# A state-space layer between two feed-forward layers: dt inside the projection, and a scan with its decays made another way

## What is computed

```python
zxbcdt = h @ w_in                              # 1024 -> 2048 (z) + 4096 (x, B, C) + 32 (dt)
xbc = silu(causal_dwconv(xbc, conv_w, conv_b))
dt = softplus(dt + dt_bias);  A = -exp(A_log)
for each chunk of 128 tokens:
    acum = cumsum(dt * A)
    lmat = exp(where(mask, acum[l] - acum[s], -inf))
    y_diag = einsum(C·B * lmat, x * dt)
    y_off = einsum(C, state) * exp(acum)
    state = state * exp(acum[-1]) + einsum(B, x * dt * exp(acum[-1] - acum))
y = (y_diag + y_off + x * D) * silu(z)
y = rms_norm(y per group of 256 channels) * norm_g
out = y @ w_out
```

## Time and profile before

| | us |
|---|---|
| median of 3 runs (lowest to highest) | 3338.79 (3338.55 to 3340.55) |
| the profiled execution, its own time | 3345.62 |
| its span, first to last instruction | 3343.8 |
| mean granted TensorE clock | 0.933 |
| TensorE busy | 3082.7 (92%) |
| VectorE busy | 2405.0 (72%) |
| ScalarE busy | 1660.4 (50%) |
| GpSimd busy | 123.0 (4%) |

### The profile page before, as it was taken

The page is one execution under the profiler, slowest core; times in us unless marked ns, Lnnn a source line. Parts: engine busy times, 40 slices in busy tenths (PEclk is TensorE's granted clock), DMA queues, the critical chain, the costliest instruction groups (busy, mean ns, idle before and its releaser), DMA issues. The chain is left out here.

```text
span 3343.8 us, 58689 instructions
## 1 busy us (share of the span) xinstructions
PE 3082.7 (92%) x23865; PEld 2754.2 (82%) x23865; DVE 2405.0 (72%) x3656; ACT 1660.4 (50%) x2382; POOL 123.0 (4%) x178
## 2 busy tenths in 40 slices
PE   7679999899888899999988899999999998988899
PEld 6567778689877789898976899899789898878798
DVE  6569999688775468787577578786578788674555
ACT  4437777554552354544552444544554544442444
POOL 0010000000102000000000000000000001011000
PEclk8779999899999799999986899999999999998899
DMA  9347999667410267586430377674157586300442
GB/s 382 140 170 288 400 402 373 247 262 310 178 64 4 95 249 305 219 313 265 155 137 1 120 298 281 257 306 178 74 229 306 221 314 260 116 2 3 166 182 80
DMA packets 77519, 698.09 MB, mean 209 GB/s; under 512 B 8433, under 2 KB 12657, under 8 KB 55409
## 3 DMA queue, kind: packets, MB, share of 16 engines
q1 hardware_dynamic: 30928, 525.06, 39.8%
q10 hardware_dynamic: 42912, 157.31, 12.4%
q0 software_dynamic: 3456, 12.58, 1.0%
HBM read 690.72 MB, written 4.19 MB: 208 GB/s over the span
## 5 line engine op out<-in xcount | busy, mean ns | idle before, releaser
L1075 PE MATMUL banks<-u_split,w_split 128*128 128x512 f32 x2816 | 1014.7, 403 | 23.3 <-DVE u_split L1320 21.2
L1144 ACT ACTIVATE w_split<-ring 128x1024 fp32r<-128x1024 f32 x513 | 541.4, 1058 | 672.6 <-PE banks L1076 408.8
L1251 DVE TENSOR_TENSOR w_split<-ring,w_split 128x1024 fp32r<-128x1024 f32 x513 | 625.9, 1223 | 293.9 <-ACT w_split L1144 290.0
L1076 PE MATMUL banks<-u_split,w_split 128*128 128x256 f32 x2816 | 797.0, 283 | 0.0
L1075 PEld LDWEIGHTS banks<-u_split,w_split 128*128 128x128 f32 x2816 | 536.8, 191 | 159.3 <-issue 17.6
L1076 PEld LDWEIGHTS banks<-u_split,w_split 128*128 128x128 f32 x2816 | 539.6, 192 | 0.0
L1067 PE MATMUL banks<-h_split,w_split 128*128 128x256 f32 x1408 | 400.7, 285 | 7.5 <-DVE w_split L1251 7.5
L1068 PE MATMUL banks<-h_split,w_split 128*128 128x256 f32 x1408 | 400.4, 284 | 0.0
L1069 PE MATMUL banks<-h_split,w_split 128*128 128x256 f32 x1408 | 400.3, 284 | 0.0
L521 PE MATMUL banks<-bufs_split,ring_split 128*128 128x256 f32 x1376 | 397.3, 289 | 0.0
L585 DVE CUSTOM_DVE_ANT_0 bufs<-bufs 128x1024 f32<-128x1024 f32 x300 | 357.0, 1224 | 12.0 <-DVE w_split L1251 12.0
(11 more groups left out here) (497 smaller groups left out, 4872.4 us busy)
## 6 DMA issues: line engine op xcount, KB each, us to landing
ring<-stream SPq DMA_DIRECT2D x155, 3072.0 KB, 11.0
bufs<-ada ACTq DMA_DIRECT2D x296, 512.0 KB, 10.7
bufs<-ada POOLq DMA_DIRECT2D x23, 512.0 KB, 6.6
bufs<-ada SPq DMA_DIRECT2D x3, 2048.0 KB, 16.0
ring<-stream SPq DMA_DIRECT2D x2, 2688.0 KB, 9.0
bufs<-c_rows SPq DMA_DIRECT2D x9, 512.0 KB, 4.4
ring<-stream SPq DMA_DIRECT2D x1, 2704.0 KB, 13.1
ring<-stream SPq DMA_DIRECT2D x1, 2176.0 KB, 8.4
```

The lines of the kernel that those rows point to most:

```text
L1075: pe.matmul(bank.rearrange("p (a t) -> p a t", a=2), w_high, u_split[:, k, :, :], start=(k == 0), stop=False, skip_group_check=True)
L1076: return pe.matmul(bank[:, 0:SEQ], w_low, u_split[:, k, 0, :], start=False, stop=(k == KC - 1), skip_group_check=True)
L1144: nc.scalar.activation(w_split[:, slot, 0, :], piece(j, b), ACT.Copy).then_inc(high.sem, 1)
L1251: e = nc.vector.tensor_tensor(w_split[:, slot, 1, :], piece(j, b), w_split[:, slot, 0, :].bitcast(F32), ALU.subtract)
```

## The change

In the plan the dt weights stand behind the second block of the projection instead of behind the last. The dt product is made as split products behind the first pair of blocks, and softplus, the product with A and the running sums are cut into eleven pieces that VectorE takes between the blocks. The preparation is left with the turning (six groups emptied by VectorE, four by ScalarE), an exponential of acum for the second chunk, and split copies of acum, of that exponential and of the identity. In the scan a mask of 0 and -1e30 is added on TensorE, by a product with the identity that comes before the rows, in the same bank; the exponentials read this bank and take acum by token as their bias; GpSimd multiplies x by dt, in place; one VectorE product of 1024 columns makes m, one of 512 the part from the state, both with an input in PSUM; m, the row parts and the state have two buffers; the y products alternate between the two halves of the output partitions; zero products stand at three places. Lines with only "..." mark what is left out.

```diff
-            blocks("mb_in", D, 2 * MB_INNER + 2 * MB_GROUPS * MB_STATE + MB_HEADS)
+            for j in range((MB_INNER + MB_CONV_DIM) // P):
+                plan.append((("mb_in", j), D))
+                if j == 1:
+                    plan.append((("mb_in", (MB_INNER + MB_CONV_DIM) // P), KC * MB_HEADS))
...
+def softplus_piece(core, dve, link, n, raw, bias, e, t, s, dt, a_neg, acum, exp_in, exped, acum_ready):
...
+    if n == 0:
+        link(dve.tensor_scalar(raw, core.psum[0:MB_HEADS, 7, 0:SEQ], bias, None, ALU.add))
+        dve.scalar_tensor_tensor(e, raw, -1.0, raw, ALU.mult, ALU.min).then_inc(exp_in.sem, exp_in.count(1))
+    elif n == 1:
+        dve.tensor_scalar(raw, raw, 0.0, None, ALU.max)
+        dve.wait_ge(exped.sem, exped.at(1))
+        link(dve.tensor_scalar(t, e, 2.0, None, ALU.add))
...
+        link(dve.tensor_scalar(t, dt, a_neg, -1.0, ALU.mult, ALU.mult))
+    elif n == 10:
+        for ck in range(2):
+            last = dve.tensor_tensor_scan(acum[:, ck * P:(ck + 1) * P], core.const("ones")[0:MB_HEADS, :], t[:, ck * P:(ck + 1) * P],
+                                          0.0, ALU.mult, ALU.add)
+        last.then_inc(acum_ready.sem, acum_ready.count(1))
...
+                    pe.wait_ge(dt_low.sem, dt_low.at(1))
+                    w = [part.rearrange("p (k m) -> p k m", k=KC) for part in dt_weights]
+                    for k in range(KC):
+                        last = three_products(pe, core.psum[0:MB_HEADS, 7, 0:SEQ], [part[:, k, :] for part in w],
+                                              [part[:, k, :] for part in u], k == 0, k == KC - 1)
+                    core.used(pe, ("mb_in", 2 * pairs), last, dt_sums)
...
-            w = core.weights(pe, ("mb_in", 2 * pairs)).rearrange("p (k m) -> p k m", k=KC)
-            for part in range(2):
-                for k in range(KC):
-                    last = pe.matmul(core.psum[0:MB_HEADS, 7, 0:SEQ], w[:, k, :], u[part][:, k, :].bitcast(F32),
-                                     start=(part == k == 0), stop=(part == 1 and k == KC - 1))
-            core.used(pe, ("mb_in", 2 * pairs), last, projected)
...
+            act.wait_ge(core.loaded[unit % SLOTS].sem, 16 * (unit // SLOTS + 1))
+            act.activation(dt_weights[0], core.ring[:, unit % SLOTS, at:at + n], ACT.Copy).then_inc(dt_high.sem, dt_high.count(1))
...
+                if g == 3:
+                    act.wait_ge(exp_in.sem, exp_in.at(1))
+                    act.activation(a_neg, core.col("mb_A_log")[0:MB_HEADS, :], ACT.Exp)
+                    act.activation(e, e, ACT.Exp).then_inc(exped.sem, exped.count(1))
...
+            dve.wait_ge(dt_high.sem, dt_high.at(1))
+            dve.tensor_tensor(dt_weights[1], core.ring[:, unit % SLOTS, at:at + n], dt_weights[0].bitcast(F32), ALU.subtract)\
+                .then_inc(dt_low.sem, dt_low.count(1))
...
+                if b == 6:
+                    dve.wait_ge(dt_sums.sem, dt_sums.at(1))
+                if b == 6 or 10 <= b < 20:
+                    softplus_piece(core, dve, link, max(b - 9, 0), dt_raw, core.col("mb_dt_bias")[0:MB_HEADS, :], e, t, s, dt, a_neg, acum,
...
-                    pe.wait_ge(turned_sb.sem, turned_sb.at(n - 6))
+                    pe.wait_ge(turned_vector.sem, turned_vector.at(n - 6))
...
+            pe.wait_ge(decay_ready.sem, decay_ready.at(1))
...
-            for n, (src, dst, ck, q) in enumerate(groups):
+            act.activation(row_exp, acum[:, P:2 * P], ACT.Exp).then_inc(row_high.sem, row_high.count(1))
+            act.activation(acum_split[0:H, :], acum, ACT.Copy).then_inc(acum_high.sem, acum_high.count(1))
+            act.wait_ge(row_high.sem, row_high.at(1))
+            act.activation(row_split[0:H, :], row_exp, ACT.Copy).then_inc(row_high.sem, row_high.count(1))
+            act.activation(ident_split, ident, ACT.Copy)
+            for half in range(2):
+                act.activation(pick[half * H:(half + 1) * H, :], ident[half * H:(half + 1) * H, half * H:(half + 1) * H], ACT.Copy)
+            for n in range(6, 10):
                 act.wait_ge(turned.sem, turned.at(n + 1))
-                act.activation(dst[:, ck, 4 * q * P:4 * (q + 1) * P], core.psum[:, n % 7, :], ACT.Copy)\
-                    .then_inc(turned_sb.sem, turned_sb.count(1))
+                act.activation(tokens(n), core.psum[:, n % 7, :], ACT.Copy).then_inc(turned_scalar.sem, turned_scalar.count(1))
...
+            dve.tensor_scalar(hidden, core.const("causal")[:, P:2 * P], -1.0, -NEG, ALU.add, ALU.mult)
+            for n in range(6):
+                dve.wait_ge(turned.sem, turned.at(n + 1))
+                dve.tensor_copy(tokens(n), core.psum[:, n % 7, :]).then_inc(turned_vector.sem, turned_vector.count(1))
+            dve.wait_ge(acum_high.sem, acum_high.at(1))
+            dve.tensor_tensor(acum_split[H:2 * H, :], acum, acum_split[0:H, :].bitcast(F32), ALU.subtract)
+            dve.wait_ge(row_high.sem, row_high.at(2))
+            dve.tensor_tensor(row_split[H:2 * H, :], row_exp, row_split[0:H, :].bitcast(F32), ALU.subtract)
             dve.wait_ge(dt_tokens.sem, dt_tokens.at(1))
-            dve.tensor_copy(by_token, core.psum[:, 7, 0:5 * H])
+            dve.tensor_copy(by_token[:, 0:2 * H], core.psum[:, 7, 0:2 * H])
+            dve.tensor_scalar(by_token[:, 2 * H:4 * H], core.psum[:, 7, 2 * H:4 * H], -1.0, None, ALU.mult)
+            dve.tensor_copy(by_token[:, 4 * H:5 * H], core.psum[:, 7, 4 * H:5 * H])
...
+        heads = lambda g: slice(4 * g, 4 * g + 4)
+
+        @block.gpsimd
+        def _(pool):
+            for g in range(MB_GROUPS):
+                rows_of = x_tok[:, :, 4 * g * HEAD:4 * (g + 1) * HEAD].rearrange("p a (h n) -> p a h n", h=4)
+                pool.tensor_tensor(rows_of, rows_of, dt[:, :, heads(g)].unsqueeze(3).to_broadcast([P, 2, 4, HEAD]), ALU.mult)\
+                    .then_inc(sig["x_weighed"].sem, sig["x_weighed"].count(1))
 
         @block.tensor
         def _(pe):
-            def pairs_and_rows(g):
+            def rows_hidden(g):
+
+                if g >= 2:
+                    pe.wait_ge(sig["decays"].sem, sig["decays"].at(g - 1))
+                for h in (0, 2):
+                    pe.matmul(core.psum[:, (1, 6)[g % 2] + h // 2, :], ident_split, hidden.unsqueeze(1).to_broadcast([P, 4, P]),
+                              start=True, stop=False, skip_group_check=True)
+                for h in range(4):
+                    last = pe.matmul(rows[g % 2][:, h, :, :], pick[:, 4 * g + h:4 * g + h + 1].to_broadcast([2 * H, P]), acum_split,
+                                     start=False, stop=True, skip_group_check=True)
+                last.then_inc(sig["row_sums"].sem, sig["row_sums"].count(1))
+            def pairs_and_parts(g):
 
                 if g:
-                    pe.wait_ge(sig["cb_sb"].sem, sig["cb_sb"].at(g))
+                    pe.wait_ge(sig["m_sb"].sem, sig["m_sb"].at(g))
+                    pe.wait_ge(sig["cs_sb"].sem, sig["cs_sb"].at(g))
                 for a in range(2):
                     now = slice(a * P, (a + 1) * P)
-                    last = pe.matmul(core.psum[:, 0, now], b[:, g, now], c_[:, g, now], start=True, stop=True)
+                    last = pe.matmul(cb_bank[:, now], b[:, g, now], c_[:, g, now], start=True, stop=True)
                 last.then_inc(sig["cb_sums"].sem, sig["cb_sums"].count(1))
-                if g >= 2:
-                    pe.wait_ge(sig["diffs"].sem, sig["diffs"].at(g - 1))
-                    pe.wait_ge(sig["rows_exp"].sem, sig["rows_exp"].at(g - 1))
                 for h in range(4):
-                    last = pe.matmul(rows[g % 2][:, h, :, :], core.const("ident")[0:H, 4 * g + h:4 * g + h + 1].to_broadcast([H, P]), acum,
+                    last = pe.matmul(part_bank[:, h, :], pick[:, 4 * g + h:4 * g + h + 1].to_broadcast([2 * H, P]), row_split,
                                      start=True, stop=True)
-                last.then_inc(sig["row_sums"].sem, sig["row_sums"].count(1))
+                last.then_inc(sig["row_parts"].sem, sig["row_parts"].count(1))
...
-            pairs_and_rows(0)
+            rows_hidden(0)
+            pairs_and_parts(0)
             state_sums(0)
-            pairs_and_rows(1)
+            rows_hidden(1)
+            keep_busy(core, pe, 4, 8)
             for g in range(MB_GROUPS):
                 if g + 1 < MB_GROUPS:
                     state_sums(g + 1)
-                pe.wait_ge(sig["m_sb"].sem, sig["m_sb"].at(g + 1))
-                pe.wait_ge(sig["cs_sb"].sem, sig["cs_sb"].at(g + 1))
+                    pairs_and_parts(g + 1)
+                else:
+                    pe.wait_ge(sig["m_sb"].sem, sig["m_sb"].at(g + 1))
+                    pe.wait_ge(sig["cs_sb"].sem, sig["cs_sb"].at(g + 1))
                 pe.wait_ge(sig["state_sb"].sem, sig["state_sb"].at(g + 1))
+                pe.wait_ge(sig["x_weighed"].sem, sig["x_weighed"].at(g + 1))
                 if g:
```

(66 more changed lines are left out.)

159 lines of the change are left out of this document (54 added, 105 removed).

## The result

The changed kernel takes **3301.74 us** (median of 4 runs, 3298.14 to 3302.67) where the kernel before takes 3339.16 (4 runs, 3338.55 to 3340.55): a ratio of 0.9886, 95% interval 0.9874 to 0.9897, or 37.4 us less. The forecast was 3302.8.

What follows compares the result with a forecast made beforehand. TensorE was taken to bound the projection, VectorE and TensorE the scan in turns, by the granted clock. Terms +0.4 - 9.5 - 8.9 - 16.5 - 1.5 = -36.0 us gave 3302.8 us; range 3294 to 3320.

Steps and rivals of the forecast that it cites:

- Projection (+0.4): Projection: the moved dt product adds 2.9 us on TensorE, the end wins only 2.5; net +0.4 us.
- Preparation (-9.5): Preparation before the scan: TensorE's transposes, then by-token copies, take 6.5 us where 16.0 stood; -9.5 us.
- forty transposes are 4.6 us at the full clock: Preparation: TensorE's time for forty transposes, 4.6 us, scaled from 28 that took 3.25.
- Start of the scan (-8.9): Scan until the first y product ends: about 8.0 us in place of 16.9; -8.9 us.
- The seven periods (-16.5): Scan, between the eight y products: 5.7 us each in place of 8.06, TensorE becoming the bound; -16.5 us.
- two thirds of the time at the full clock: Scan periods: TensorE's assumed clock share, 5.0 us per group at full and 9.1 at low clock, giving 5.9.
- rival C: Scan: TensorE never waits and stays at full clock, periods 4.9 us, 3297 or a little less; chance 0.08.
- The tail (-1.5): Scan after the last y product: squares and spreading at full clock save 0.8 and 0.7 us; -1.5 us.
- A: Scan: the clock stays as mixed as before, periods of 7.2 us; -23 us, 3316; chance 0.28.
- B: Scan: the clock is low throughout, periods of 9.4 us; -5 us, 3334; chance 0.07.
- D: Scan: groups stop overlapping, 12.4 us per group at 1.2 GHz; slower, 3355 us; chance 0.02.
- E: Preparation: stays at 10 us or more because by-token copies wait; 3306 us; chance 0.55 together with the forecast.

Runs made afterwards that it cites:

- second profile of before: The kernel before, run again with no edit, a single run: 3332.03 us.
- experiment 8: Changed kernel plus twenty zero products of 512 columns behind the projection's last block: 3300.54 us; also without the tail's zeros 3298.41, without all nineteen 3296.31.
- second pair of profiles: Repeats with no edit, of the kernel before (3332.03 us, single run) and of the changed kernel (3302.43 us, 4 runs).
- experiment 6: Changed kernel with each group's square sums issued twice, a single run: 3317.44 us.

## Why the prediction was right, step by step

The time was right to 1 us, by errors of both signs that cancelled: that much is luck. So is part of the size: the periods were counted from a profile with a group of 10.96 us. From the second profile of before the same 5.7 per period would have been -13.0 and not -16.5.

**Projection (+0.4):** right. -0.3 and +0.15 in two profiles; the end went from the dt product to the SiLU, and the softplus pieces and table loads cost nothing.

**Preparation (-9.5): mis-sized by 0.7 to 2.** The 8.8 us wait for the softplus went, as said, and the way through TensorE is the longest. The step that failed is "forty transposes are 4.6 us at the full clock". I had seen that the SiLU chain stays behind the last block, and had not asked what TensorE does meanwhile: it idles 5.46 us and the clock falls. The transposes took 7.33 and 6.08 us. At the full clock they took 4.56, and the stage 5.76 (experiment 8), below the forecast's 6.5.

**Start of the scan (-8.9): missed by 2.0 and 5.1.** At the full clock and without the zeros it is 9.09, against 8.0. Three terms were short. The change's eight zero products, which I had placed in waits "that are there anyway", delay the second group's state and pairs by 0.9. GpSimd's contention, entered as nothing, hides behind them, and is worth up to 0.7 without them (an estimate from 1.16 and 0.42 us). And VectorE takes the second group's product and the third weighing before it adds, 0.7 where the list had a handover of 0.1. In the rows, the instruction with two SBUF inputs went from 0.42 us to between 0.75 and 1.25 beside GpSimd, while those that read PSUM stayed at 0.69 and 1.21. By the Trainium skill's rule (SBUF — State Buffer, Who interferes with whom), a shared port locked for the whole instruction, with two SBUF inputs as the condition, it should be so, and the trace agrees. The rest is the clock: +13.05 where it fell.

**The seven periods (-16.5): missed by 6 on the good side (by 4 in the second pair of profiles).** The mechanism was right: VectorE from 7.46 to 3.9, TensorE the bound, VectorE waiting for it. The failed step is "two thirds of the time at the full clock": it was 1.00, but for one dip at 1768 in one profile. That made rival C's case true for the groups, with periods of 4.64 to 4.81 (its 4.9), not the forecast's 5.7. Inside, the mask and rows were 1.31 and not 1.0, the parts 0.59 and not 0.25: the narrow fp32r products cost 0.15 us each, 0.06 was taken because 256 columns cost 0.12, and the price hardly falls with the columns. Pairs, squares and state came 0.3 cheaper together, y at 1.46 lay between its ends. The steady group is then 5.33, just above the 4.8 to 5.3 of my list; but the first two periods are without squares (4.45) and the last has neither rows nor state, pairs and parts (2.6 to 2.8), which I had not counted.

**The tail (-1.5):** -0.95. Squares and spreading did speed up, the zeros in front of them took 0.7 back against the best end without them (12.25); against the worst, with the clock down from the last squares on (13.81), they gave 0.9.

**Rivals.** A and B (a mixed or low clock in the groups) did not happen; the mixed clock with twice the squares shows that they could have. C's mechanism held in the groups, its time was spoilt by the start. D did not: from 1740 to 1768 TensorE had no idle time. E did not: the copies by token ended 8.3 us after the stage's start.

What stays open: why the clock stays up in a steady group, fell there for 3 us in one profile and fell with doubled squares; why it fell once or twice at the start of otherwise equal kernels; and how the gain per group divides between VectorE's relief and TensorE's shorter list.

## What to carry to other kernels

Find the engine that has no gap between two ends of a group before the clock is blamed: filling the clock under the old order gave 2.0 to 5.5 us of the periods, the other 17 to 18.5 came with the new order, in which VectorE's floor of 7.46 us is gone and TensorE's list is the bound at 5.33. That order needs the clock too: at a mixed one, with the doubled squares, its groups took 8.3 to 8.6 us (experiment 6). When work is taken from the end of a stage, ask what TensorE does in the time that it leaves: 5.5 us of idle cost the next two stretches 2.8 to 4.6 us, and 20 zero products there, not at the places where the engine is already busy, brought it back. Fillers are instructions too: each of the nineteen others stood in front of something. The eight at the scan's head cost 0.9 us; with the eleven of the tail the end was 12.95 to 12.97, without them it varied from 12.25 to 13.81.

## What had not been expected of the hardware

- An fp32r product of 128 columns with a broadcast column of weights takes 0.15 us at the full clock (four in 0.59), one of 256 columns 0.16 (four in 0.65), where the projection's products of 256 columns take 0.12. Half the columns saved 0.01 us.
- TensorE's clock fell to 0.50 in a stretch where it counted as busy for 8.00 of 8.00 us, when products of one column were doubled. It was at 1.00 for 28 us in the same groups with half of them, with and without zero products at their head, and then fell for 3 us in one of these profiles, with TensorE busy for 6.00 of 6.00 us. One profile of the doubled products doesn't show that they were the cause.
- The old order of the 24 y products costs 1.73 us, the alternating one 1.46, where 0.055 us per record, as elsewhere, would give 1.3.
- The clock came up inside a row of nothing but transposes. TensorE in the changed kernel's preparation, by stretch:

```profile
1723.50:1726.00 2.50, 2.50 (x14) 2.50 (x13) 2.02 (x4) 0.83 (x5) 0.00 (x0) 0.50 0.00 0
1726.00:1728.50 2.50, 2.50 (x20) 2.50 (x18) 1.95 (x4) 1.03 (x3) 0.00 (x0) 0.78 0.00 0
```

The forty transposes began at 1721.41 after the idle time and had the engine to themselves; behind the 20 zeros they ran at 1.00 from the first to the last. The Trainium skill (TensorE: Matmul & The Clock Gate, Part 4: PE-mode transpose) says that the full clock doesn't come in for products in the engine's transpose mode. The trace calls these records MATMUL and doesn't show whether they use that mode; if they do, it disagrees with the page, and the trace decides.
